# mLSTM memory cells: banks released one by one, one sum of squares on VectorE, a ones column in the values, states ahead of the norm

## What is computed

```python
q, k, v = x @ w_q, x @ w_k, x @ w_v            # from 2048 features
s   = (q @ k.T) * exp(d_intra - m_t)
num = w_inter * (q @ C) + s @ v
den = w_inter * (q @ n) + sum(s)
h   = num / max(abs(den), exp(-m_t))
kw  = k * g_rows
C_new = g_state * C + kw.T @ v                 # matrix memory, 128 x 256
n_new = g_state * n + sum(kw)                  # normaliser
h   = h * rsqrt(mean(h * h) + eps) * g_mh      # norm over the head's 256 features
```

## Time and profile before

| | |
|---|---|
| median of three timed runs | 3052.49 us |
| profiled execution | 3051.82 us |
| its span, first to last instruction | 3050.3 us |
| TensorE busy | 2920.4 us, 96% of the span |
| VectorE, ScalarE busy | 1560.3 us (51%), 1074.5 us (35%) |
| DMA | 139 GB/s over the span |
| mean granted TensorE clock | 0.981 of full speed |

### The profile page before, as it was taken

The page is one execution under the profiler, slowest core; times in us unless marked ns, Lnnn a source line. Parts: engine busy times, 40 slices in busy tenths (PEclk is TensorE's granted clock), DMA queues, the critical chain, the costliest instruction groups (busy, mean ns, idle before and its releaser), DMA issues.

```text
span 3050.3 us, 49093 instructions
## 1 busy us (share of the span) xinstructions
PE 2920.4 (96%) x18542; PEld 2765.6 (91%) x18542; DVE 1560.3 (51%) x2021; ACT 1074.5 (35%) x1267; POOL 78.6 (3%) x119
## 2 busy tenths in 40 slices
PE   8999598999999999998999999998999999999997
PEld 5777498999999999998788888998999999999997
DVE  1899946544433444445654544446544433444444
ACT  3223454433333333333333233344333333333333
POOL 2110000000000000000000000000000000000000
PEclk9999799999999999999999999999999999999999
DMA  6334143444444444444243535444444444444442
GB/s 176 125 124 124 49 147 119 150 147 151 149 148 151 150 147 151 148 150 138 76 144 116 161 108 164 136 148 127 146 151 148 148 152 148 148 151 148 148 152 90
DMA packets 374564, 423.30 MB, mean 139 GB/s; under 512 B 27034, under 2 KB 302210, under 8 KB 374114
## 3 DMA queue, kind: packets, MB, share of 16 engines
q1 hardware_dynamic: 367776, 399.61, 41.2%
q0 software_dynamic: 5744, 22.21, 2.4%
q10 hardware_dynamic: 960, 0.38, 0.1%
HBM read 409.22 MB, written 14.31 MB: 139 GB/s over the span
## 4 chain that ended last, share of the span: by engine, by line
PE 84%; DVE 12%; issue 2%; ACT 2%; DMA 0%; DVEq 0%; ACTq 0%; SPq 0%
PE PS L1415 26%; PE PS L1416 26%; PE PS L1417 26%; DVE branch L978 7%; PE PS L1413 1%; DVE lo L889 1%; DVE branch L1010 1%; DVE C L1346 1%; PE PS L1668 0%; PE PS L1661 0%; PE PS L1686 0%; ACT sq L679 0%; PE PS L1448 0%; PE PS L1621 0%; DVE branch L974 0%
## 5 line engine op out<-in xcount | busy, mean ns | idle before, releaser
L889 DVE TENSOR_TENSOR lo<-raw,hi 128x1024 fp32r<-128x1024 f32 x688 | 842.3, 1225 | 1140.9 <-ACT hi L561 1140.7
L1415 PE MATMUL PS<-xh,hi 128*128 128x320 f32 x4096 | 1283.9, 313 | 64.1 <-issue 34.0
L1416 PE MATMUL PS<-xl,hi 128*128 128x320 f32 x4096 | 1275.5, 311 | 0.0
L1417 PE MATMUL PS<-xh,lo 128*128 128x320 f32 x4096 | 1275.1, 311 | 0.0
L561 ACT ACTIVATE hi<-raw 128x1024 fp32r<-128x1024 f32 x688 | 724.7, 1057 | 1176.5 <-PE PS L1417 1176.5
L1415 PEld LDWEIGHTS PS<-xh,hi 128*128 128x128 f32 x4096 | 776.9, 190 | 81.4 <-issue 46.4
L1416 PEld LDWEIGHTS PS<-xl,hi 128*128 128x128 f32 x4096 | 777.3, 190 | 0.0
L1417 PEld LDWEIGHTS PS<-xh,lo 128*128 128x128 f32 x4096 | 776.3, 190 | 0.0
L1417 PE MATMUL PS<-hh,lo 128*128 128x320 f32 x1408 | 435.8, 310 | 0.0
L1416 PE MATMUL PS<-hl,hi 128*128 128x320 f32 x1408 | 435.8, 310 | 0.0
L1415 PE MATMUL PS<-hh,hi 128*128 128x320 f32 x1408 | 435.8, 310 | 0.0
(11 more groups left out here) (277 smaller groups left out, 1310.6 us busy)
## 6 DMA issues: line engine op xcount, KB each, us to landing
raw<-in_ffn_w_gate SPq DMA_DIRECT2D x352, 256.0 KB, 2.8
raw<-in_ffn_w_up SPq DMA_DIRECT2D x352, 256.0 KB, 3.0
raw<-in_ffn_w_down SPq DMA_DIRECT2D x352, 256.0 KB, 3.3
raw<-in_conv_w_pw SPq DMA_DIRECT2D x192, 256.0 KB, 2.9
raw<-in_mlstm_w_v SPq DMA_DIRECT2D x64, 256.0 KB, 3.1
raw<-in_mlstm_w_out SPq DMA_DIRECT2D x64, 256.0 KB, 3.2
raw<-in_mlstm_w_q SPq DMA_DIRECT2D x64, 128.0 KB, 2.2
raw<-in_mlstm_w_k SPq DMA_DIRECT2D x64, 128.0 KB, 2.4
```

The costliest lines, as they stand in the source:

```text
L889: v.tensor_tensor(lo[:, slot, :, :], raw[:, slot, :, :], hi[:, slot, :, :].bitcast(F32), ALU.subtract).then_inc(lo_done, 1)
L1415: mm(out, hi[:, slot, kk, cols], rhs_hi[:, k, :], start=begin, stop=False, skip_group_check=True)
L1416: mm(out, hi[:, slot, kk, cols], rhs_lo[:, k, :], start=False, stop=False, skip_group_check=True)
L1417: ins = mm(out, lo[:, slot, kk, cols], rhs_hi[:, k, :], start=False, stop=end, skip_group_check=True)
```

## The change

There are five edits.

1. The four banks of a head are released one by one. VectorE counts each evacuation of q, k and the first half of v in a new semaphore `qkv_read` (three a head), the second half of v stays with `banks_read`. TensorE's first unit of the next group waits for its bank ahead of each column block, not for all four ahead of the unit.
2. On VectorE all four evacuations stand together in window 7: q, k, then the row table `head_out`, then v; the `split` of window 7 follows them.
3. VectorE adds the two halves of the squares (`cell_squares`, semaphore `hq_add`), and TensorE's `cell_norm` sums them with one product in place of two.
4. The value tile `v_tok` is one column wider, and that column holds ones, set once by GpSimd. The two `kw` by `v_tok` products yield the prompt's normaliser as column 257, and the two products against a column of ones are gone.
5. On VectorE the updates of state pairs 0 and 1 move to window 4, behind the squares' sum and ahead of the norm; the norm (`cell_norm`) moves to window 5.

```diff
-        v_tok = cell("v_tok", [P, 3, DV])
+        v_tok = cell("v_tok", [P, 3, DV + 1])
...
+            g.memset(v_tok[:, :, DV:DV + 1], 1.0)
...
                 v.scalar_tensor_tensor(out=qT[:, :], in0=PS[:, 0, 0:T], scalar=float(DK) ** -0.5, in1=rx[:, :],
-                                       op0=ALU.mult, op1=ALU.mult)
+                                       op0=ALU.mult, op1=ALU.mult).then_inc(qkv_read, 1)
                 wait_bank(dve, ph["qkv"], h, 1)
-                v.tensor_tensor(kT[:, :], PS[:, 1, 0:T], rx[:, :], ALU.mult)
+                v.tensor_tensor(kT[:, :], PS[:, 1, 0:T], rx[:, :], ALU.mult).then_inc(qkv_read, 1)
...
-                    last = v.tensor_tensor(vT[:, i, :], PS[:, 2 + i, 0:T], rx[:, :], ALU.mult)
-                last.then_inc(banks_read, 1)
+                    v.tensor_tensor(vT[:, i, :], PS[:, 2 + i, 0:T], rx[:, :], ALU.mult).then_inc(
+                        banks_read if i else qkv_read, 1)
...
+            def cell_squares(h):
+                dve.wait_ge(hq_sq, h + 1)
+                v.tensor_tensor(sq[:, 1, 0, :], sq[:, 0, 0, :], sq[:, 0, 1, :], ALU.add).then_inc(hq_add, 1)
...
-            def cell_before(h, last=False, first_head=False):
-                return {0: [lambda: v_out(h)] if not first_head else [], 1: [lambda: cell_top(h)], 3: [lambda: cell_den(h)],
-                        4: [lambda: cell_norm(h)], 5: [lambda: cell_state(h, 0), lambda: cell_state(h, 1)],
-                        6: [lambda: cell_state(h, 2)],
-                        7: [lambda: cell_state(h, 3)] + ([] if last else [lambda: head_out(h + 1), lambda: qk_out(h + 1)])}
+            def cell_before(h, last=False):
+                return {1: [lambda: cell_top(h)], 3: [lambda: cell_den(h)],
+                        4: [lambda: cell_squares(h), lambda: cell_state(h, 0), lambda: cell_state(h, 1)],
+                        5: [lambda: cell_norm(h)], 6: [lambda: cell_state(h, 2)],
+                        7: [lambda: cell_state(h, 3)] + ([] if last else [
+                            lambda: qk_out(h + 1), lambda: head_out(h + 1), lambda: v_out(h + 1)])}
...
                 for m in range(BANKS):
+                    if free is not None:
+                        pe.wait_ge(*free(m))
...
-                if not isinstance(g, int) or glob >= 2:
+                free = None
+                if single and not (p is ph["qkv"] and isinstance(g, int) and g == 0):
+                    heads = g if p is ph["qkv"] else H
+                    free = lambda m: (qkv_read, heads * 3 + (m - 2)) if m < BANKS - 1 else (banks_read, glob)
+                elif not isinstance(g, int) or glob >= 2:
                     pe.wait_ge(banks_read, glob if single else glob - 1)
...
-                pe.wait_ge(hq_sq, h + 1)
-                mm(PS[:, 6, 0:T], ones[:, :], sq[:, 0, 0, :], start=True, stop=False, skip_group_check=True)
-                mm(PS[:, 6, 0:T], ones[:, :], sq[:, 0, 1, :], start=False, stop=True, skip_group_check=True).then_inc(hq_sum, 1)
-                mm(PS[:, 4, 0:DV], kw[:, 0, :], v_tok[:, 0, :], start=True, stop=False, skip_group_check=True)
-                mm(PS[:, 4, 0:DV], kw[:, 1, :], v_tok[:, 1, :], start=False, stop=True, skip_group_check=True)
-                mm(PS[:, 4, DV:DV + B], kw[0:TS, 2, :], seg[:, :], start=False, stop=True, skip_group_check=True)
-                mm(PS[:, 4, DV + B:DV + B + 1], kw[:, 0, :], ones[:, 0:1], start=False, stop=False, skip_group_check=True)
-                mm(PS[:, 4, DV + B:DV + B + 1], kw[:, 1, :], ones[:, 0:1], start=False, stop=True, skip_group_check=True).then_inc(Cp_done, 1)
+                pe.wait_ge(hq_add, h + 1)
+                mm(PS[:, 6, 0:T], ones[:, :], sq[:, 1, 0, :], start=True, stop=True, skip_group_check=True).then_inc(hq_sum, 1)
+                mm(PS[:, 4, 0:DV + 1], kw[:, 0, :], v_tok[:, 0, :], start=True, stop=False, skip_group_check=True)
+                mm(PS[:, 4, 0:DV + 1], kw[:, 1, :], v_tok[:, 1, :], start=False, stop=True, skip_group_check=True)
+                mm(PS[:, 4, DV + 1:DV + 1 + B], kw[0:TS, 2, :], seg[:, :], start=False, stop=True,
+                   skip_group_check=True).then_inc(Cp_done, 1)
```

More of the change, by code:

```diff
@@ L277, in trunk_kernel @@
             sem(n) for n in ("gate_mm", "row_dve", "row_act", "row_turned", "row_cols", "n0_turned"))
-        fold_ready = sem("fold_ready")
+        fold_ready, qkv_read, hq_add = sem("fold_ready"), sem("qkv_read"), sem("hq_add")
         masks_ready, w_if_ready = sem("masks_ready"), sem("w_if_ready")
@@ L821, in cell_top @@
                 act.wait_ge(kv_turned, h + 1)
-                s.activation(v_tok[:, 0:2, :], PS[:, 5, :].rearrange("p (t v) -> p t v", t=2), ACT.Copy).then_inc(v_ready, 1)
+                s.activation(v_tok[:, 0:2, 0:DV], PS[:, 5, :].rearrange("p (t v) -> p t v", t=2), ACT.Copy).then_inc(v_ready, 1)
             def cell_den(h):
@@ L1310, in cell_top @@
                     v.tensor_scalar(kw[:, t, :], PS[:, 4, t * P:(t + 1) * P], col(gr_tok, t), None, ALU.mult)
-                v.tensor_copy(v_tok[0:TS, 2, :], PS[0:TS, 4, 2 * P:4 * P]).then_inc(kw_ready, 1)
+                v.tensor_copy(v_tok[0:TS, 2, 0:DV], PS[0:TS, 4, 2 * P:4 * P]).then_inc(kw_ready, 1)
                 dve.wait_ge(kw_ready, h * 2 + 2)
@@ L1338, in cell_norm @@
                 dve.wait_ge(Cp_read, h + 1)
-                v.tensor_tensor(n_head(n_new), tC[:, 0, 0:B], Cn_prm[:, DV:DV + B], ALU.add)
-                v.tensor_copy(n_new[:, bass.ds(h + B * H, 1)], Cn_prm[:, DV + B:DV + B + 1]).then_inc(n_done, 1)
+                v.tensor_tensor(n_head(n_new), tC[:, 0, 0:B], Cn_prm[:, DV + 1:DV + 1 + B], ALU.add)
+                v.tensor_copy(n_new[:, bass.ds(h + B * H, 1)], Cn_prm[:, DV:DV + 1]).then_inc(n_done, 1)
             def cell_state(h, pair):
@@ L1357, in _ @@
             window(p, 0, split, before)
-            window(p, 1, split, cell_before(0, first_head=True))
+            window(p, 1, split, cell_before(0))
             with dve.Fori(2, p.groups) as w:
@@ L1397, in _, with unit @@
             mm, turn = nc.tensor.matmul, nc.tensor.transpose
-            def unit(p, g_bank, j, slot, quad, n, rhs_hi, rhs_lo):
+            def unit(p, g_bank, j, slot, quad, n, rhs_hi, rhs_lo, free=None):
                 if p is ph["pw1"]:
@@ L1434, in group @@
                     n = g * p.units + (p.unit0 + j)
-                    unit(p, b, j, u % SLOTS, g * (p.units // SLOTS) + j // SLOTS, n, *rhs)
+                    unit(p, b, j, u % SLOTS, g * (p.units // SLOTS) + j // SLOTS, n, *rhs, free=None if j else free)
                 for f in before.get(p.units, []):
@@ L1686, in state_pair @@
                     ins = mm(PS[:, 5 + 2 * i, pair % 2 * DV:(pair % 2 + 1) * DV], kw_seq[tokens, pair + B // 2 * i, :],
-                             v_tok[tokens, 2, :], start=pair % 2 == 0, stop=True, skip_group_check=True)
+                             v_tok[tokens, 2, 0:DV], start=pair % 2 == 0, stop=True, skip_group_check=True)
                 ins.then_inc(Cs_done, 1)
             def cell_norm(h):
-                pe.wait_ge(hq_sq, h + 1)
-                mm(PS[:, 6, 0:T], ones[:, :], sq[:, 0, 0, :], start=True, stop=False, skip_group_check=True)
-                mm(PS[:, 6, 0:T], ones[:, :], sq[:, 0, 1, :], start=False, stop=True, skip_group_check=True).then_inc(hq_sum, 1)
-                mm(PS[:, 4, 0:DV], kw[:, 0, :], v_tok[:, 0, :], start=True, stop=False, skip_group_check=True)
-                mm(PS[:, 4, 0:DV], kw[:, 1, :], v_tok[:, 1, :], start=False, stop=True, skip_group_check=True)
-                mm(PS[:, 4, DV:DV + B], kw[0:TS, 2, :], seg[:, :], start=False, stop=True, skip_group_check=True)
-                mm(PS[:, 4, DV + B:DV + B + 1], kw[:, 0, :], ones[:, 0:1], start=False, stop=False, skip_group_check=True)
-                mm(PS[:, 4, DV + B:DV + B + 1], kw[:, 1, :], ones[:, 0:1], start=False, stop=True, skip_group_check=True).then_inc(Cp_done, 1)
+                pe.wait_ge(hq_add, h + 1)
[4 more added lines that the diff above has]
+                   skip_group_check=True).then_inc(Cp_done, 1)
                 state_pair(h, 0)
```

## The result

The changed kernel took **3018.33 us** (median of four runs, 3017.78 to 3020.77) against 3052.47 us for the kernel before (four runs, 3045.44 to 3055.36): a ratio of 0.9897, 95% interval 0.9879 to 0.9915. The forecast was 3020.0. The profiled execution of after took 3018.86 us, with a span of 3017.3 us; the one of before took 3051.82 us.

The account below looks back on a forecast made before the run. TensorE was taken as the bound, except the last 11 us of a head, where VectorE is. 8.6 + 2.1 + 15.5 + 1.1 + 5.2 = 32.5 us saved gave 3020.0 us against the median, range 3014 to 3030.

Parts of the forecast that it names:

- VectorE's chain: End of each head: state products to q out takes 9.78 us, leaving TensorE waiting 0.42 instead of 2.63; saves 15.5 us.
- TensorE's side: Same stretch of a head on TensorE, first state products to the group's end: 9.36 us.
- The semaphore between the engines: Signal from VectorE to TensorE at a head's end, taken as 0.13 us.
- banks 1 to 3: Next head's first unit: k and v come out before TensorE needs their banks, so these cost nothing.
- Saved products: Sum of squares 0.54 and ones column 0.53 us, together 1.07 in each of 8 heads: 8.6 us.
- the states' wait: TensorE's 0.35 us wait for VectorE's state updates goes with states ahead of the norm: 6 x 0.35 = 2.1 us.
- The clock: Heads' loop: shorter waits leave no half-clock spells, 4 x 1.3 = 5.2 us; called the softest term.
- The rival that the spells stay: Heads' loop: half-clock spells have another cause, so 5.2 us are not won: 3025.2 us; chance 0.11.
- Products on `v_tok`: Rival in the loop: unaligned rows slow these 46.5 us of products; at twice the time 3066 us; chance 0.03 (slower).
- The row that spoke against it: Evidence against slower `v_tok` products: 16 products with stationary `u_new`, rows 376 bytes apart, all take 272 to 273 ns.
- The cover of the reload: States' reload in the loop: there at 14.5 us, wanted by TensorE at 17.3, so 2.8 us of cover.
- Met waits: Three more TensorE waits in a head's first unit, each bounded by 0 and 0.1 us, taken as 0.

Follow-up runs that it names:

- products_only: Kernel before plus only the one-product sum of squares and the ones column (edits 3 and 4); 3046.99 us, ratio 0.9994.
- norm_first: Changed kernel with edit 5 undone, the norm ahead of state pairs 0 and 1 on VectorE; 3020.11 us.
- release_only: Kernel before plus only banks released one by one and the four evacuations together (edits 1 and 2); 3026.68 us, ratio 0.9920.
- q_first: Changed kernel with the evacuations of q and k ahead of the last pair of state updates on VectorE; 3015.61 us, ratio 0.9886.
- before_a: Kernel before, unchanged, profiled again; an execution of the lower cluster of times, 3046.12 us.
- before_b: Kernel before, unchanged, profiled again; an execution of the upper cluster of times, 3053.74 us.

## Why the prediction was right

*VectorE's chain.* Forecast 9.78 us from the state products to TensorE's start; 1627.28 - 1617.56 = 9.72. TensorE's side: forecast 9.36, measured 9.46, since the second pair of states' products starts 0.24 us behind a unit's last product (1622.34 - 1622.10), 0.1 more than a unit's spacing. So TensorE was 0.26 us late, not 0.42. Over the seven boundaries it lost 1.7 us where 2.9 were forecast: the term was mis-sized, and 1.2 us more were won. The semaphore between the engines took 0.06 us here, half of what was taken. Behind a boundary the unit's products stand 0.15 us apart from the second on, so banks 1 to 3 cost nothing, as forecast.

*Saved products and the states' wait.* The products gave 1.07 us a head, as forecast. The states' wait of 0.35 was worth 0.42: in before these products start 1633.80 - 1633.14 = 0.66 us behind the unit's last, in after 0.24. The row of before that stands ahead of the wait in the earlier trace rows:

```profile
1633.14 0.31 PE L1417 MATMUL PS<-xh,lo 128*128 128x320 f32 x1
```

With 2.37 us won at five boundaries and 2.21 at the last, the six distances have 6 x (1.07 + 0.42) + 5 x 2.37 + 2.21 = 23.0 us without the clock, and with its 5.6 (below) 28.6 of the 28.63. But the terms are not independent, as it was put: `products_only` and `norm_first` show that without edit 5 the ones column's 0.53 would come back as a wait. Nor was the last cell: its wait for `vrows` grew from 0.85 us to 1.19, so it won 0.82, not 1.07.

*The clock.* Four spells were to go, at 1.3 us; they went. Before's four heads with one are 48.20 us on average against 46.79, so 1.4 each, 5.6 in all, where 5.2 were forecast. The prediction counted four behind six waits; the loop has seven of these waits, and the seventh had none. The rival that the spells stay did not come about: `release_only`, `norm_first`, `q_first` and both profiles of the change, where a head's first product is at most 0.35 us late, have no spell there, and the states' wait of 0.87 us in `norm_first` has none behind it. The rule that the prediction cited from the Trainium skill (TensorE: Matmul & The Clock Gate, "Why this matters for your kernels"), read as a bound below which the clock holds, would have kept them; these runs disagree with it.

*Products on `v_tok`.* All products with this tile, after (columns as in the earlier trace rows):

```profile
1492.00:1845.00 353.00, 46.50 (x256) 32.56 (x256) 3.25 (x8) 4.82 (x8) 0.00 (x0) 0.98 0.45 139
```

46.50 us against 46.47: the rival's price is nothing. The row that spoke against it was of a stationary operand, while in the two wide products `v_tok` is the moving one; it is the row after that settles it.

*The cover of the reload.* This was right for the head shown and too large for most others, without harm. The list of DMA issues, and GpSimd's queue and TensorE in after, which answer:

```profile
C<-in_state_C POOLq DMA_DIRECT2D x8, 1024.0 KB, 7.3
```

```profile
1636.04 0.90 POOL L515 DMA_DIRECT2D C<-in_state_C  x1 [6.92 <-DMA out_C_sample<-C]
...
1644.62 0.65 PE L1680 MATMUL PS<-C,qw_seq 128*64 128x256 f32 x4
```

This reload landed 5.9 us after its issue, at 1641.9, and was wanted at 1644.62: 2.7 us of cover, where 2.8 was forecast. But the median to landing is 7.3 us where it was 6.2, and the loop's seven reloads had 0.9 to 2.7 us of cover, 1.4 in the median. `q_first` wants the states earlier and used up most of that.

*Met waits.* Three more in a head's first unit were bounded by 0 and 0.1 each. In `q_first` all four are met, and all products of that unit stand 0.15 us apart; so they cost nothing there that can be seen.

*What was luck.* The loop won 34.1 us where 32.5 were forecast, and the rest of the span, which no edit touches, lost 1.1: so the sum came out nearer than its terms. And the profile that the forecast starts from, of 3051.82 us, has the slow stretch at 1507 us, as after's has. From the 3046.12 us of `before_a` the same 32.5 us would have given 3013.6, 4.7 below what was measured.

## What to carry to other kernels

When two engines take turns at the same buffers, measure from one common event how long each one's chain is to the point of meeting, and put first in the longer chain what the other one waits for. A product saved on the engine that waits is worth nothing until the chain that it waits for ends earlier too, as with the ones column here. When an unchanged kernel's times fall into clusters, compare executions of the same cluster, by their profiles. Short stalls between dense products can cost more than their length through the clock, so count the stretches behind a wait by their granted clock.

## What the runs showed of the hardware that was not expected

The half clock behind a short wait is neither certain nor the same from head to head: with waits of 2.5 us, four of seven had a spell in each of five profiles of before, and six of seven in `products_only`; with 2.99 us, six of seven; with 1.86 us, two of seven in one execution and none in the next; with the states' 0.87 us in `norm_first` and the 0.35 us and less at the boundaries of after, none. A spell cost 1.3 to 1.6 us. What decides on a single head stays open. The same holds of the stretch at 1507 us, which ran at the lower level in three of before's five profiles (granted 0.53 to 0.55 over 7 us) and at full clock in the other two. Between `before_a` and `before_b` it makes 3.2 of 7.6 us, so it is a large part of the 3045 to 3055 us over which an unchanged kernel's times spread.
